# The last mixer of a two-block transformer: weight units by heads, and stick-breaking in pairs of heads between half units of the in-projection

## The reference, cut to what matters

```python
def odd_mixer(h, w_in, w_out):                       # h: 256 tokens x 1024
    q, k, v = jnp.split(h @ w_in, 3, axis=-1)        # w_in 1024 x 3072
    o = stick_breaking(q, k, v)                      # 16 heads of 64
    return o.reshape(B_, S, SB_W) @ w_out

def stick_breaking(q, k, v):                         # per head, z = q.k / 8
    causal = s < t
    log_beta = jax.nn.log_sigmoid(z)
    log_1mb = jnp.where(causal, jax.nn.log_sigmoid(-z), 0.0)
    acc = lax.cumsum(log_1mb, axis=3, reverse=True) - log_1mb
    a = jnp.where(causal, jnp.exp(log_beta + acc), 0.0)
    return a @ v
```

## Time and profile before

| what | value |
|---|---|
| median of 3 runs | 2288.6 us (2285.0 to 2290.29) |
| profiled execution, its span | 2288.3 us |
| TensorE busy in the span | 2211.3 us, 97% |
| in-projection of the last mixer, units 1 to 11 | 65.02 us |
| stick-breaking, until the out-projection starts | 53.65 us |
| out-projection of the last mixer | 24.45 us |

### The profile page before, as it was taken

One profiled execution on the slowest core, in us unless ns is written; L12 is line 12 of the kernel. 1 busy time (PEld: TensorE's weight loads), 2 busy tenths in 40 slices (PEclk: granted clock), 3 DMA queues, 4 the chain that ended last, 5 costly groups with the idle time before them and its releaser, 6 DMA issues.

```text
span 2288.3 us, 35915 instructions
## 1 busy us (share of the span) xinstructions
PE 2211.3 (97%) x15182; PEld 2013.6 (88%) x15182; DVE 1593.6 (70%) x1774; ACT 1130.4 (49%) x1436; POOL 6.7 (0%) x16
## 2 busy tenths in 40 slices
PE   9999999999999999989999979999999999999998
PEld 7888888768999999989999948889998978899897
DVE  4896686346777777648775446888887445888887
ACT  4222231345434444444344445677776455677775
POOL 0000000000000000000000000000000000000000
PEclk9999999999999999999999989999999989999999
DMA  8577867514887788537885512888886412788885
GB/s 313 192 238 245 281 231 259 197 56 165 307 293 276 262 288 309 181 131 277 304 300 184 184 38 93 294 308 300 295 318 233 162 59 93 260 295 301 317 307 213
DMA packets 126741, 535.53 MB, mean 234 GB/s; under 512 B 11744, under 2 KB 47912, under 8 KB 82416
## 3 DMA queue, kind: packets, MB, share of 16 engines
q1 hardware_dynamic: 124896, 524.33, 64.3%
q0 software_dynamic: 944, 5.72, 0.6%
q10 hardware_dynamic: 736, 3.10, 0.4%
HBM read 532.04 MB, written 1.06 MB: 233 GB/s over the span
## 4 chain that ended last, share of the span: by engine, by line
PE 87%; DVE 8%; ACT 3%; issue 1%; DMA 1%; DVEq 0%; ACTq 0%; SPq 0%
PE PS L904 16%; PE PS L1352 13%; PE PS L830 11%; PE PS L976 9%; PE PS L1386 7%; PE PS L926 7%; PE PS L865 5%; PE PS L1031 4%; DVE moe_low L2495 3%; PE PS L1310 2%; PE PS L1288 1%; PE PS L731 1%; PE PS L799 1%; PE PS L964 1%; ACT W_HIGH L1830 1%
## 5 line engine op out<-in xcount | busy, mean ns | idle before, releaser
L904 PE MATMUL PS<-h_parts,FFN_HIGH 128*128 128x256 f32 x2112 | 383.1, 284 | 2.9 <-DVE h_parts L2063 2.9
L2495 DVE TENSOR_TENSOR moe_low<-moe_ring,W_HIGH 128x2048 fp32r<-128x2048 f32 x128 | 292.9, 2290 | 76.7 <-ACT W_HIGH L1830 76.7
L904 PEld LDWEIGHTS PS<-h_parts,FFN_HIGH 128*128 128x128 f32 x2112 | 329.0, 192 | 3.7 <-issue 3.4
L904 PE MATMUL PS<-h_parts,ring_low 128*128 128x256 f32 x1056 | 298.7, 283 | 0.0
L1352 PE MATMUL PS<-moe_low,HXH 128*96 128x256 f32 x1008 | 282.7, 281 | 0.0
L1830 ACT ACTIVATE W_HIGH<-moe_ring 128x2048 fp32r<-128x2048 f32 x128 | 244.7, 1913 | 22.9 <-PE PS L1386 21.8
L2090 DVE TENSOR_TENSOR ring_low<-ring,FFN_HIGH 128x2048 fp32r<-128x2048 f32 x99 | 226.8, 2291 | 41.3 <-ACT FFN_HIGH L1604 41.1
L2121 DVE SCALAR_TENSOR_TENSOR roots<-CB,cond_rows,roots 128x1024 f32<-128x1024 f32 x186 | 238.4, 1282 | 8.9
L1604 ACT ACTIVATE FFN_HIGH<-ring 128x2048 fp32r<-128x2048 f32 x99 | 189.1, 1910 | 103.3 <-DMA ring<-down_w 89.6
L904 PEld LDWEIGHTS PS<-h_parts,ring_low 128*128 128x128 f32 x1056 | 202.6, 192 | 0.0
L1352 PEld LDWEIGHTS PS<-moe_low,HXH 128*96 128x96 f32 x1008 | 164.2, 163 | 0.3
(11 more groups left out here) (353 smaller groups left out, 5034.9 us busy)
## 6 DMA issues: line engine op xcount, KB each, us to landing
moe_ring<-moe_w SPq DMA_DIRECT2D x192, 1024.0 KB, 5.0
CB<-mod_rows SPq DMA_DIRECT2D x192, 512.0 KB, 6.0
ring<-up_w SPq DMA_DIRECT2D x88, 1024.0 KB, 5.0
ring<-lin_w SPq DMA_DIRECT2D x55, 1024.0 KB, 4.9
ring<-down_w SPq DMA_DIRECT2D x43, 1024.0 KB, 6.0
CB<-mod_dual SPq DMA_DIRECT2D x96, 128.0 KB, 2.7
ring<-mod_w SPq DMA_DIRECT2D x8, 1024.0 KB, 8.1
CB<-mod_rows SPq DMA_DIRECT2D x32, 128.0 KB, 3.0
```

The costliest lines, as they stand in the source:

```text
L904: return mm(PS[:, i % 2, h * S:(h + 1) * S], a[:, k, h * P:(h + 1) * P], b[:, k, :], start=start, stop=(k == KT - 1 and j == 2), skip_grou ...
L2495: tt(by_tile(moe_low[:, moe_slot(l, p), :]), by_tile(moe_ring[:, moe_slot(l, p), :]), w_high_tiles(p), ALU.subtract).then_inc(w_low, 1)
```

## The change

The units of `o_in` come in the order of the heads that they serve: q, k of heads 0 to 3, q, k of heads 4 to 7, v of heads 0 to 3, and so on. Heads go in pairs p (heads 2p, 2p+1, which lie on rows 0 to 63 and 64 to 127 of a tile of `O_QK`). The program runs in 28 steps: step n < 24 is a half unit (n // 2, half n % 2) into bank 6 or 7, and behind it, where the tables say so, come the output, the sums and the scores of a pair. VectorE's and ScalarE's instructions handle a pair at once, 768 columns instead of 384; z and a lie in `CB` (4 pairs), l in `SG` (2 pairs). The high parts have three buffers, and the parts of unit n // 2 + 2 are made in step n. The scores of the two heads stand alternately on the two row halves of the array, the output products on its two column halves, and each group signals once, at its end.

```diff
+O_UNITS = (("q", 0), ("k", 0), ("q", 1), ("k", 1), ("v", 0), ("q", 2), ("k", 2), ("v", 1), ("q", 3), ("k", 3),
+           ("v", 2), ("v", 3))
+O_SCORES = (4, 6, 9, 11, 14, 16, 20, 21)
+O_SUMS = tuple(n + 3 for n in O_SCORES)
+O_OUT = (10, 11, 16, 17, 22, 23, 25, 26)
...
+        O_HIGH = (IN_HIGH[1], rounded("O_HIGH", late_at, [P, UW])[:, :], IN_HIGH[0])
...
-            stream("o_in", 12, lin_w, LIN0["o_in"], peel=1)
+            for i, (kind, c) in enumerate(O_UNITS):
+                load(UNIT0["o_in"] + i, 0, 0, UNIT0["o_in"] + i + 1, UW, source(lin_w, LIN0["o_in"] + O_FIRST[kind] + c))
...
+                def half_unit(i, c):
+                    bank = 6 + i % 2
+                    if c == 0:
+                        pe.wait_ge(w_low, SPLIT0["o_in"] + i + 1)
+                        if i >= 2:
+                            pe.wait_ge(lin_ready, t0 + i - 1)
...
+                def pair_scores(p):
+                    pe.wait_ge(lin_ready, t0 + O_AT["k", p // 2] + 1)
+                    if p:
+                        pe.wait_ge(sb_z, p)
+                    for cut, keys, queries in ((slice(0, S), slice(0, P), slice(0, S)), (slice(S, S + P), slice(P, S), slice(P, S))):
+                        for half in range(2):
+                            rows = slice(64 * half, 64 * half + 64)
+                            last = mm(PS[:, half, cut], O_QK[rows, 8 + p, keys], O_QK[rows, p, queries], start=True, stop=True)
+                    last.then_inc(sb_scores, 1)
+                def pair_sums(p):
+                    pe.wait_ge(sb_l, p + 1)
+                    if p:
+                        pe.wait_ge(sb_w, p)
+                    for half in range(2):
+                        lm = by_head(o_work("l", p))[:, half, :]
+                        mm(PS[:, 2 + half, 0:S], tab("upper"), lm[:, 0:S], start=True, stop=False)
+                        mm(PS[:, 2 + half, P:S], tab("ones"), lm[:, S:S + P], start=False, stop=True)
+                        last = mm(PS[:, 2 + half, S:S + P], tab("upper"), lm[:, S:S + P], start=True, stop=True)
+                    last.then_inc(sb_sums, 1)
+                def pair_out(p):
+                    pe.wait_ge(lin_ready, t0 + O_AT["v", p // 2] + 1)
+                    pe.wait_ge(sb_a, p + 1)
+                    if p >= 2:
+                        pe.wait_ge(sb_kept, p - 1)
+                    a = by_head(o_work("z", p))
+                    for t, cut, keys in ((0, slice(0, S), slice(0, S)), (1, slice(P, S), slice(S, S + P))):
+                        for half in range(2):
+                            at = 128 * p + 64 * half
+                            last = mm(PS[64 * half:64 * half + 64, 4 + p % 2, cut], O_V[:, t, at:at + 64], a[:, half, keys],
+                                      start=(t == 0), stop=(t == 1), skip_group_check=True)
+                    last.then_inc(sb_out, 1)
+                for n in range(O_STEPS):
+                    if n < 24:
+                        half_unit(n // 2, n % 2)
+                    if n in O_OUT:
+                        pair_out(O_OUT.index(n))
+                    if n in O_SUMS:
+                        pair_sums(O_SUMS.index(n))
+                    if n in O_SCORES:
+                        pair_scores(O_SCORES.index(n))
...
+                split_o(1)
+                for n in range(O_STEPS):
+                    if n % 2 == 0 and 2 <= n <= 24:
+                        evacuate_o(n // 2 - 1)
+                    if n - 1 in O_OUT:
+                        kept(O_OUT.index(n - 1))
+                    if n - 1 in O_SUMS:
+                        weights(O_SUMS.index(n - 1))
+                    if n - 1 in O_SCORES:
+                        softplus(O_SCORES.index(n - 1))
+                    if n % 2 == 0 and n // 2 + 2 < 12:
+                        split_o(n // 2 + 2)
...
+                split_in("o_in", (1,))
+                for n in range(O_STEPS):
+                    if n - 1 in O_SCORES:
+                        masked(O_SCORES.index(n - 1))
+                    if n - 1 in O_SUMS:
+                        exponents(O_SUMS.index(n - 1))
+                    if n % 2 == 0 and n // 2 + 2 < 12:
+                        split_in("o_in", (n // 2 + 2,))
+                    if n - 1 in O_SCORES:
+                        logs(O_SCORES.index(n - 1))
```

More of the change, by code:

```diff
@@ L466, in in_high @@
         def in_high(name, i):
-            return by_tile(FFN_HIGH[2 + i] if i < 2 and name != "o_in" else IN_HIGH[(i + 1) % 2])
+            if name == "o_in":
+                return by_tile(O_HIGH[i % 3])
+            return by_tile(FFN_HIGH[2 + i] if i < 2 else IN_HIGH[(i + 1) % 2])
         def scratch(at, *shape):
@@ L1209, in mixer_o @@
             def mixer_o():
[L1210 to L1245, removed]
@@ new lines, in mixer_o @@
+                t0 = LIN_TILE0["o_in"]
+                def half_unit(i, c):
[4 more added lines that the diff above has]
+                            pe.wait_ge(lin_ready, t0 + i - 1)
+                    if i == 0:
+                        last = lead_products("o_in", 8, bank) if c == 0 else None
+                    else:
+                        moves = O_UNITS[i][0] == "v"
+                        last = in_products("o_in", i, 0, PS[:, bank, c * S:(c + 1) * S], moves, slice(c * P, (c + 1) * P))
+                    if last is not None and (c or i == 0):
+                        last.then_inc(unit_done, 1)
@@ L1785, in mixer_o @@
             def mixer_o():
[L1786 to L1810, removed]
@@ L2383, in mixer_o, with masked, logs, exponents @@
             def mixer_o():
[L2384 to L2400, removed]
+                def masked(p):
+                    dve.wait_ge(sb_scores, p + 1)
+                    if p >= 4:
+                        dve.wait_ge(sb_out, p - 3)
+                    tt(by_head(o_work("z", p)), PS[:, 0:2, 0:384], tab("after").unsqueeze(1).to_broadcast([P, 2, 384]), ALU.add)\
+                        .then_inc(sb_z, 1)
+                def logs(p):
+                    z, l = o_work("z", p), o_work("l", p)
+                    dve.wait_ge(sb_log, p + 1)
+                    stt(out=l, in0=z, scalar=0.0, in1=l, op0=ALU.max, op1=ALU.add).then_inc(sb_l, 1)
+                def exponents(p):
+                    z = by_head(o_work("z", p))
+                    dve.wait_ge(sb_sums, p + 1)
+                    tt(z, z, PS[:, 2:4, 0:384], ALU.subtract).then_inc(sb_w, 1)
+                split_in("o_in", (1,))
[8 more added lines that the diff above has]
+                        logs(O_SCORES.index(n - 1))
                 add_out("o_out", 192, 2, 9)
```

50 lines of the change are left out of this document (44 added, 6 removed).

## The result

The changed kernel takes **2268.1 us** (median of 4 runs, 2265.84 to 2269.36) against 2288.8 us (4 runs, 2285.0 to 2290.29) of the kernel before on the same chip: ratio 0.9911, 95% interval 0.9899 to 0.9923, so 20.7 us less (18 to 23). The forecast was 15.1 us less, at 2273.5 us.

What follows compares the result with a forecast made beforehand. TensorE, busy 97%, was taken to bound the kernel. In-projection 65.0 + products 29.4 + stalls 7.7 + clock 1.5 = 103.6 against 118.67 us, 15.1 less: 2273.5 us from 2288.6, range 2269 to 2278 (chance 0.57).

Steps and rivals of the forecast that it cites:

- rival B: Pairs don't overlap or stalls double: 10.4 us more products, stage 111 us, time 2281 us (2278 to 2284); chance 0.17.
- C: ScalarE and VectorE run strictly in turn; out-projection starts 10 us later than now, 2299 us; chance 0.06.
- D: Order changed but nothing won, since TensorE at 97% gives no room: 2288 us; chance 0.03.
- rival A: ScalarE's and VectorE's queues keep up, shorter stalls, no half clock: stage 96.0 us, time 2266 us (below 2269); chance 0.17.
- The filling and the thin part at 0.50: Start of stick-breaking before: 4.50 us of filling, then 15.69 us at granted clock 0.50; both were to go.
- The drain: End of stick-breaking, 2.52 us before; pair 7's sums to wait 1.0, its output 1.1, CAT copy 0.45 us.
- Products, 29.4 us: Stick-breaking's products on TensorE, two heads of a pair overlapping in the array: 29.4 us against 43.4.
- Change of tiling: Each switch of the part of the array in use costs 0.14 to 0.20 us; 28 switches, before about 48.
- Stalls, 7.7 us: TensorE's waits for in-order ScalarE and VectorE queues, mid-stage and in the drain: 7.7 us together, bounds 1.6 and 13.
- step 14: Sums of pair 3, late because VectorE's logarithms stand behind unit 8's low half: TensorE waits 2.0 us.
- step 16: Output of pair 2, held by ScalarE's late evacuation of unit 7 (v1): TensorE waits 3.1 us.
- Clock, 1.5 us: Half clock after a 3.1 us stall amid dense products, charged once at 1.5 us; bounds 0 and 5.

Runs made afterwards that it cites:

- e7_same_half: Changed kernel with both heads of a pair on the same half of the array, same number and shapes of products: 2277.5 us, ratio 0.9948.
- e5_split_first: Changed kernel with ScalarE's high part of a unit ahead of the softplus of the same step instead of behind it: 2266.3 us, one run.
- e1_serial: Changed kernel with a pair's scores and output products issued head after head instead of alternately: 2267.8 us, ratio 0.9911.
- e2_behind: Changed kernel with all eight pairs behind the in-projection, sums one step and output two behind the scores: 2323.0 us, ratio 1.0171.
- e8_behind_lag: Changed kernel with all pairs behind the in-projection, sums two steps and output four behind the scores: 2287.1 us, ratio 0.9993.
- e3_spare: Kernel before with 21 unused 128-column products in idle places at the start of stick-breaking: 2283.0 us, ratio 0.9985.

## Why the prediction was right

The mechanism held: 18.0 us left the stage where 15.1 were forecast, and rivals B, C and D fell. The point forecast came out within 5.4 us, but the median of 2268.1 lies just inside rival A's band (below 2269, chance 0.17) and not in the forecast's own; the later median of 2270.3 lies in the latter. Half of A came true, since no clock was lost, and the waits in the middle were shorter but there.

- **Bound.** TensorE's work sets most of the stage before and after (busy 95.08 of 100.64 us). The filling and the thin part at 0.50 went, as forecast. The drain did not: it had 0.9 us of idle (2.52 with 1.64 busy; the prediction's 1.7 is a misreading, but enters no sum) and has 2.8 now.
- **Products, 29.4 us.** The stage's busy time of 95.08 less the in-projection's 65.0 is 30.1. By rows: 8 x (0.85 + 0.80) + 6 x 1.74 + 2 x 1.94 for the sums + ten returns into a half unit at 0.20 = 29.5. e7_same_half shows that the two halves of the array do it: 10.0 us of busy time if they are not used, where rival B had 10.4, with 2.6 swallowed by the waits where it had some 3. The other 3.3 of the 13.3 us fit the 20 changes of tiling fewer (28 instead of 48) at 0.14 to 0.20, an estimate that no run tests by itself.
- **Change of tiling.** Confirmed in both directions: 0.43 against 0.63 at the head of the sums, 3.06 against 2.86 for a half unit.
- **The other engines.** 0.95 and 0.84 for 768 elements were forecast, 0.950 to 0.957 and 0.840 to 0.845 measured.
- **Stalls, 7.7 us: the mis-sized term.** Each came at its forecast place with its forecast releaser, but step 14 took 0.6 instead of 2.0 and step 16 took 2.2 instead of 3.1; the drain's 1.1, 1.2 and 0.5 are as forecast (1.0, 1.1, 0.45). Together 5.56. My layout added up durations and put handovers between them; the chain shows instructions of one queue following each other in less. At 1825.72 VectorE's takes 0.87 of the chain and the next starts, and in the group its mean is 0.957. Over the five or six such instructions ahead of each place that is an estimate of some 0.5 us. Against the layout, moved to this trace's start of unit 1, the inputs came 1.0 us early at step 14 and 1.6 at step 16. TensorE came 0.5 us later than laid out at step 14, and so waited 1.4 less; at step 16 it came 0.7 earlier, and so waited 0.9 less. What beyond the 0.5 us made the two queues early is open.
- **Clock, 1.5 us: it cost 0.** The stretch at 0.50 is unit 1's start, 3.09 us here and 3.16 before, which is in the 65.0. The window of the stage has a mean of 0.98, as the in-projection before, and this window, which begins ahead of the wait of 2.2 us and ends a whole half unit behind it, has 1.00:

```profile
1836.00:1850.00 14.00, 11.82 (x98) 10.58 (x97) 5.94 (x5) 9.79 (x13) 0.00 (x0) 1.00 0.34 126
```

  The idle ahead of unit 1 (2.6 us) was a poor model for a wait of 2.2 inside dense work.

So 65.0 + 30.1 + 5.56 + 0 = 100.6, 3.0 less than 103.6: products 0.7 more, waits 2.1 less, clock 1.5 less. The first error hid a part of the other two. The other 2.7 us of the measured 20.7 are outside the stage and not the change's.

What A describes was one edit away: e5_split_first, one helper call moved, brings the stage to 97.5 where A had 96.0.

## What to carry to other kernels

Before you make products cheaper, look at what sets the pace behind them: here the overlap of two heads was worth 7.45 us between half units, and pairing behind the in-projection 0.2 us, because there the chain of ScalarE and VectorE, in the order written, took 6.1 us a pair. Another order might have given more. When a serial pipeline is laid between steps of a dense one, write out all in-order queues side by side and look for an instruction that both engines' later work hangs on (here the high part of a weight unit): move that ahead of the long elementwise chain. Judge such a change by the length of its stage, since executions of the same code ahead of it differ too: here by up to 9.7 us in unit 1's start.

## What the runs showed of the hardware

- Two fp32 heads overlap in the array in either order of issue: 0.85 and 0.80 alternating, 0.86 and 0.81 one behind the other, 1.50 and 1.45 on the same half. This holds for the two column halves too, where all 128 rows are in use by both. With one head written behind the other, the second head's first product still starts 0.013 us behind the first head's (e1_serial), where the first head alone takes 0.65.
- Weight loads run beside products whether or not the two use the same part of the array. In e7_same_half, all on one column half, eight loads lie within the time of their eight products (timeline, loads and then products):

```profile
1869.71 1.27 PEld L1280 LDWEIGHTS PS<-CB,G 128*64 128x64 f32 x8
1869.72 1.51 PE L1280 MATMUL PS<-CB,G 128*64 128x256 f32 x8
```

  The Trainium skill, TensorE: Matmul & The Clock Gate, section Part 3: Packing small matmuls, says that a weight load overlaps running products only where the row groups differ. These two rows don't agree with that; the measurement decides. So what the halves add, 0.80 against 1.45, is that the products of two heads run at once.
- A wait of 2.2 us amid dense products left the granted clock at 1.00, while a pipeline with waits in every pair had 0.63 (e2_behind) and 0.87 (e8_behind_lag) on average.
- 21 spare products in the thin filling of the kernel before kept the clock at 1.00 (e3_spare). That took 6.6 to 6.9 us off the other products, and with the spares' own time 3.15 us off the stage.
